# Modulation tiles stored transposed and summed on VectorE, the opening and the load order rearranged, narrow projections merged

## The chip, the cores and the metric

The kernel runs on one core of a Trainium2 chip, in one launch. The metric is the device time of a launch in microseconds (us). The core's engines run side by side and synchronise by semaphores: TensorE (PE, matmuls into PSUM), VectorE (DVE), ScalarE (ACT), GpSimd (POOL), and SyncE (SP), which here issues every DMA, in the order of the program.

## What is computed

Two small transformer blocks of float32, on 256 tokens of width 1024. The first has two layers whose norms are modulated by a condition vector `c`; the second adds 16 meta tokens, a differential attention and 16 experts.

```python
cond = jax.nn.silu(c)
for layer in range(2):
    mod = cond @ ada_w[layer] + ada_b[layer]                  # (1024) x (1024, 6144)
    sh1, sc1, g1, sh2, sc2, g2 = jnp.split(mod, 6, axis=-1)
    h = modulate(rms_norm(x, mix_norm[layer]), sh1, sc1)      # y * (1 + sc1) + sh1
    y = ab_mixer(h, ...) if layer == 0 else cd_mixer(h, ...)
    x = x + g1 * y
    h = modulate(rms_norm(x, ffn_norm[layer]), sh2, sc2)
    x = x + g2 * swiglu(h, ffn_w1[layer], ffn_w2[layer])
# then second_block(x, ...): attention and convolution, 16 experts of 34 tokens each
```

In `ab_mixer`, `h @ w_in` gives gated linear attention inputs (`gq, gk, gv`, a gate of rank 16, `gr`), attention inputs (`dq, dk, dv`), and an indexer (`iq` with 8 heads, one shared key `ik` of 64, and 8 weights `iw` per token). The indexer's scores pick 64 keys per token; q and k are normed and rotated; the outputs are projected back.

## The kernel before

Everything is kept transposed, features on partitions and tokens along the free dimension: `X` and `H` are 8 tiles of 128 x 272, of which 256 columns are the tokens. Weights come through a ring of five slots `RING_T` of 2 MB each (128 x 4096). The list `LOADS` fixes which weight goes into which slot: entry j takes slot j mod 5. `sp_weight` (L2314) issues a load on SP after it has waited until the slot's last user is done (`w.prev.left`); since SP is one queue, a load that waits also holds up all loads behind it.

The 6144 modulation values of a layer are made in 12 tiles of 512, `("ada", layer, i)`: tiles 0 and 1 are the shift of the first norm, 2 and 3 its scale, 4 and 5 the gate of the mixer, 6 and 7 the shift of the second norm, 8 and 9 its scale, 10 and 11 the gate of the FFN. A tile holds 8 groups of 128 inputs x 512 outputs. `dve_ada` multiplies each group by the silu of `c` (one value per partition, `CND`) and adds into `ACC` (L1610, then L1613). Then `pe_ada` sums over the partitions with four matmuls against a column of ones (L473, 16 instructions for two tiles), and `dve_mod` adds the bias from PSUM (L1623). For the first four tiles PE takes the last group itself (L506).

The order of the work is written out by hand for each engine, in `pe_ab`, `act_ab`, `dve_ab`, `pool_ab` and in `sync_program`. In the opening, VectorE first makes the angles of the rotation (L1675 to L1696), then the four first tiles with the statistic of the first norm between them, then scales x (L1640); ScalarE adds the shift (L1167); PE does the narrow projections: gate (L519, 16 columns), the indexer key twice into two halves of the partitions (L524), gate expansion (L530), and the token weights (L535, 32 matmuls of 8 columns). Then come the wide projections in chunks of 128 outputs (`pe_chunk`, L418, 16 instructions for 256 tokens): iq, gqk, gv (L427), and then dq, dk, dv and gr between the steps of the two attentions. On VectorE the long selection of the 64 keys is L1771 and L1773, eight rounds; the scores are L1756 to L1763; norms are L1561 to L1583. The out projection (`pe_out_proj`) has a `hook` by which PE and VectorE do tiles 6 to 9 between its chunks, and the residual is L1657. The FFNs (L741 to L743 and L760 to L762) sum more tiles in between (`EXTRA`), as does the second layer's mixer.

Of the kernel before, what the change touches and what calls it, by code (L numbers as in the profile page):

```python
# [6 lines left out]
F32 = mybir.dt.float32  # L7
# [29 lines left out]
    ("ident", 128), ("ones", 128), ("rot128", 128), ("rot64", 128), ("tri16", 128), ("tri", 128),  # L37
    ("after", 128), ("before", 128), ("tmask", 128), ("smask", 128), ("cmask", 256), ("inv", 2),
    ("eps", 1), ("one", 1), ("iota", CAP),
# [3 lines left out]
    ("c", 8), ("ada_b", 96), ("mix_norm", 16), ("ffn_norm", 16), ("gla_out", 1), ("dsa_q", 1), ("dsa_k", 1),  # L43
# [50 lines left out]
def ada_steps(n):
    return KC - 1 if n < 4 else KC


def ada_done(n):
    return sum(ada_steps(i) for i in range(n % 2, n + 1, 2))
# [8 lines left out]
HS = {"mix0": 0, "ffn0": 8, "mix1": 16, "ffn1": 24}  # L108
# [115 lines left out]
def bc(ap, *shape):  # L224
# [22 lines left out]
class Kit:  # L247


    def __init__(self, nc, A, out):  # L250
# [4 lines left out]
        self.HWC = sbt("HWC", [128, KC * L + KC * SMALL + LN], F32)  # L255
# [3 lines left out]
        self.CL = self.HWC[:, KC * (L + SMALL):]  # L259
# [53 lines left out]
class AbViews:  # L313
    def __init__(self, s):
# [19 lines left out]
        self.IW = s.take(2, 8)  # L334
# [3 lines left out]
        self.G1 = self.TR[:, 3, 0:T]  # L338
        self.PT = self.bufs[0].rearrange("p a (b c) -> p (a b) c", c=128)
# [125 lines left out]
def pe_ada(nc, k, n):  # L465

    key = ("ada", *ADAS[n])
    early = n < 4
    u = k.banks[key] if early else pe_bank(nc, k, key)
    acc = k.ACC[:, n % 2, :]  # L470
    nc.tensor.wait_ge(k.sem[f"ada{n % 2}"], ada_done(n))
# [3 lines left out]
    ins.then_inc(u.full, 1)  # L475
    if early:

        k.ring[key].left = (u.full, u.n)
        k.banks.drop(key)


def pe_out_proj(nc, k, name, keys, mix, n, stat, hook):
    for i in range(2):
        w = k.ring[keys[i]]
        nc.tensor.wait_ge(w.sem, w.n)
        for j in range(4):
            u = pe_chunk(nc, k, (name, "out", 4 * i + j), w.v(KC, 512), j, mix, n)
            stat.upto(min(max(4 * i + j - stat.lag, 0), KC) if 4 * i + j < 7 else 7)
            hook(4 * i + j)
        w.left = (u.full, u.n)  # L490
    stat.upto(KC)


def pe_ab(nc, k):
    pe, s, v, P, ring = nc.tensor, k.sem, k.ab, k.banks, k.ring
    ones = k.cc("ones")
    pe.wait_ge(s["vecs"], 16)
    pe.wait_ge(s["consts"], 16)
    pe.wait_ge(s["cond"], 1)

    for n in range(4):
        w = ring["ada", 0, n]
        u = pe_bank(nc, k, ("ada", 0, n), hold=True)
        pe.wait_ge(w.sem, w.n)
        for j in range(4):
            pe.matmul(u.t[:, j:j + 1], w.v(KC, 512)[:, 7, j * 128:(j + 1) * 128], k.CND[:, 7:8],  # L506
                      start=j == 0, stop=False, skip_group_check=True)
        if n == 0:
            stat = PeStat(nc, k, "mix0", M)
            stat.upto(KC)  # L510
        else:
            pe_ada(nc, k, n - 1)
    pe_ada(nc, k, 3)

    u = pe_bank(nc, k, "g1")
    pe.wait_ge(s["small"], 16)
# [10 lines left out]
    pe.wait_ge(P["g1"].taken, P["g1"].done)  # L527
# [74 lines left out]
    pe_ada(nc, k, ADA_AT[0, 4])  # L602
    pe_ada(nc, k, ADA_AT[0, 5])
# [102 lines left out]
    pe_out_proj(nc, k, "ab", [("abo", 0), ("abo", 1)], v.MIX, T, stat, hook)  # L706
# [6 lines left out]
def pe_ffn(nc, k, layer):  # L713
# [73 lines left out]
def pe_cd(nc, k):  # L787
# [17 lines left out]
    pe_ada(nc, k, ADA_AT[1, 4])  # L805
    pe_ada(nc, k, ADA_AT[1, 5])
# [11 lines left out]
    pe_ada(nc, k, ADA_AT[1, 6])  # L818
    pe_ada(nc, k, ADA_AT[1, 7])
# [37 lines left out]
    pe_out_proj(nc, k, "cd", [("cdo", 0), ("cdo", 1)], v.MIX, T, stat, hook)  # L857


def pe_diff(nc, k):  # L860
# [1659 lines left out]
```

## Time and profile before

| | us |
|---|---|
| median of three timed runs | 1958.38 (1957.93 to 1961.32) |
| the profiled execution | 1954.44 |
| its span, first to last instruction | 1953.0 |
| PE busy (share) | 1716.3 (88%) |
| VectorE busy (share) | 642.9 (33%) |
| ScalarE busy (share) | 370.8 (19%) |
| GpSimd busy (share) | 28.8 (1%) |
| DMA, mean over the span | 295 GB/s |
| first layer's mixer ends, first FFN starts | about 245 |

Shares are means over stages with different limits, so they don't say what a stage waits for. The timeline tells when an instruction ran and, in square brackets, how long its engine had been idle and what released it; the chain of waits is followed back from the last instruction of the kernel.

### The profile page before, as it was taken

To read this page: it belongs to the slowest core of one execution; us is meant where nothing else is said; L and a number is where in the kernel's file an instruction comes from. 1 tells how busy PE (TensorE), PEld (TensorE's weight loads), DVE (VectorE), ACT (ScalarE), POOL (GpSimd) and SP (SyncE) were. 2 spreads that over 40 slices of the span, in tenths; PEclk is the share of its full clock that TensorE was granted. 3 is DMA by queue.
4 is the path that set the end of the run, shared out by engine and by line. 5 is a ranking of instruction groups with operands and counts; after the bars stand their busy time and mean duration, and the time that the engine had idled before them with its cause. 6 is when DMAs were issued, how large, how long until landed. Compare 5 with 4: busy or idle time off the path is not lost.

```text
span 1953.0 us, 21048 instructions
## 1 busy us (share of the span) xinstructions
PE 1716.3 (88%) x8993; PEld 1034.4 (53%) x8993; DVE 642.9 (33%) x1230; ACT 370.8 (19%) x649; POOL 28.8 (1%) x35
## 2 busy tenths in 40 slices
PE   4999889999989999999798889878888887797787
PEld 3776789997679999757532323222222222232222
DVE  6156678755657554344300100101001010010102
ACT  2112243333324333132100000000000000000001
POOL 0101000000000000100001000000000000000000
PEclk7999989999899999999879999989998899999989
DMA  9342457744554656123539989999999999999995
GB/s 393 139 184 87 191 219 289 313 175 173 220 194 149 250 185 237 43 96 120 215 133 413 428 363 390 425 429 428 426 426 427 428 422 428 427 422 428 426 424 243
DMA packets 43309, 576.48 MB, mean 295 GB/s; under 512 B 4673, under 2 KB 6482, under 8 KB 6866
## 3 DMA queue, kind: packets, MB, share of 16 engines
q1 hardware_dynamic: 43218, 575.15, 71.5%
q8 instruction: 72, 1.18, 0.2%
q14 instruction: 19, 0.16, 0.0%
HBM read 574.08 MB, written 1.05 MB: 294 GB/s over the span
## 4 chain that ended last, share of the span: by engine, by line
PE 68%; DMA 23%; DVE 6%; ACT 2%; issue 1%; SPq 0%; DVEq 0%; ACTq 0%
DMA RING_T<-in_w_up 22%; PE P L1046 17%; PE P L418 12%; PE P L1067 5%; PE P L741 4%; PE P L742 4%; PE P L743 4%; PE P L427 3%; PE P L760 2%; PE P L762 2%; PE P L761 2%; PE P L1025 2%; DVE ACC L1613 2%; PE P L1083 2%; PE P L445 1%; PE P L473 1%
## 5 line engine op out<-in xcount | busy, mean ns | idle before, releaser
L1046 PE MATMUL P<-RING_T,SCR 128*34 128x512 f32 x1008 | 485.2, 638 | 128.4 <-DMA RING_T<-in_w_up 128.3
L1047 PE MATMUL P<-RING_T,SCR 128*34 128x512 f32 x992 | 479.1, 640 | 0.0
L1046 PEld LDWEIGHTS P<-RING_T,SCR 128*34 128x34 f32 x1008 | 114.8, 119 | 446.1 <-issue 445.6
L2170 DVE TENSOR_TENSOR SCR<-P,SCR 34x512 f32<-34x512 f32 x64 | 44.3, 693 | 785.5 <-ACT SCR L1515 785.5
L1067 PE MATMUL P<-RING_T,SCR 128*34 128x512 f32 x512 | 230.5, 598 | 18.3 <-DMA RING_T<-in_w_down 18.3
L1068 PE MATMUL P<-RING_T,SCR 128*34 128x512 f32 x512 | 230.4, 598 | 0.0
L741 PE MATMUL P<-SCF 128*128 128x256 f32 x704 | 204.9, 291 | 15.6 <-DVE SCF L1890 10.9
L418 PE MATMUL P<-HWC,RING_T 128*128 128x256 f32 (+1 forms) x832 | 197.5, 396 | 7.9 <-ACT HWC L1167 4.1
L742 PE MATMUL P<-SCF 128*128 128x256 f32 x704 | 202.5, 288 | 0.0
L743 PE MATMUL P<-SCF 128*128 128x256 f32 x704 | 202.4, 287 | 0.0
L418 PEld LDWEIGHTS P<-HWC,RING_T 128*128 128x128 f32 x832 | 162.0, 196 | 40.9 <-issue 14.3
L1515 ACT ACTIVATE SCR<-P 34x512 f32<-34x512 f32 x64 | 37.8, 591 | 611.6 <-PE P L1047 611.6
L741 PEld LDWEIGHTS P<-SCF 128*128 128x128 f32 x704 | 138.1, 196 | 17.6 <-issue 11.7
L1067 PEld LDWEIGHTS P<-RING_T,SCR 128*34 128x34 f32 x512 | 53.6, 112 | 164.8 <-issue 123.9
L742 PEld LDWEIGHTS P<-SCF 128*128 128x128 f32 x704 | 138.7, 197 | 0.0
L743 PEld LDWEIGHTS P<-SCF 128*128 128x128 f32 x704 | 138.5, 197 | 0.0
L1867 DVE TENSOR_TENSOR SCF<-RING_T,SCF 128x1024 fp32r<-128x1024 f32 x88 | 106.1, 1221 | 39.9 <-ACT SCF L1310 39.9
L1047 PEld LDWEIGHTS P<-RING_T,SCR 128*34 128x34 f32 x992 | 113.2, 119 | 0.0
L1613 DVE SCALAR_TENSOR_TENSOR ACC<-RING_T,CND,ACC 128x512 f32<-128x512 f32 x164 | 111.6, 746 | 0.9
L1310 ACT ACTIVATE SCF<-RING_T 128x1024 fp32r<-128x1024 f32 x88 | 91.9, 1053 | 66.0 <-PE P L762 35.0
L760 PE MATMUL P<-SCF 128*128 128x256 f32 x352 | 100.7, 286 | 0.0
L761 PE MATMUL P<-SCF 128*128 128x256 f32 x352 | 99.6, 283 | 0.0
(246 smaller groups left out, 1793.8 us busy)
## 6 DMA issues: line engine op xcount, KB each, us to landing
RING_T<-in_w_down SPq DMA_DIRECT2D x64, 2048.0 KB, 13.2
RING_T<-in_w_gate SPq DMA_DIRECT2D x63, 2048.0 KB, 17.2
RING_T<-in_w_up SPq DMA_DIRECT2D x62, 2048.0 KB, 12.4
RING_T<-in_ada_w SPq DMA_DIRECT2D x24, 2048.0 KB, 12.3
RING_T<-in_ffn_w SPq DMA_DIRECT2D x22, 2048.0 KB, 8.5
RING_T<-in_ffn_w SPq DMA_DIRECT2D x22, 1024.0 KB, 4.9
RING_T<-in_ab_w_in SPq DMA_DIRECT2D x7, 2048.0 KB, 12.7
RING_T<-in_w_in SPq DMA_DIRECT2D x6, 2048.0 KB, 7.4
```

Of the source, the lines that this page charges most:

```text
L418: ins = nc.tensor.matmul(u.t[:, 0:n], wap[:, c, j * 128:(j + 1) * 128], h[:, c, :], start=c == 0, stop=c == KC - 1)
L741: pe.matmul(o, wh, v.HH[:, 0, c, :], start=c == 0, stop=False)
L742: pe.matmul(o, wh, v.HH[:, 1, c, :], start=False, stop=False)
L743: ins = pe.matmul(o, wl, v.HH[:, 0, c, :], start=False, stop=c == KC - 1)
L760: pe.matmul(o, wh, v.HR[:, f % NHD, 0, :], start=f == 0 and m % 2 == 0, stop=False, skip_group_check=True)
L761: pe.matmul(o, wh, v.HR[:, f % NHD, 1, :], start=False, stop=False, skip_group_check=True)
L1046: pe.matmul(u.t[0:CAP, :], xs, wg.v(KC, 512)[:, c, :], start=c == 0, stop=c == KC - 1)
L1047: ins = pe.matmul(u.t[64:64 + CAP, :], xs, wu.v(KC, 512)[:, c, :], start=c == 0, stop=c == KC - 1)
L1067: pe.matmul(u.t[0:CAP, :], hs, w.v(4, 1024)[:, c, 0:512], start=first, stop=end)
L1068: ins = pe.matmul(u.t[64:64 + CAP, :], hs, w.v(4, 1024)[:, c, 512:1024], start=first, stop=end)
L1613: nc.vector.scalar_tensor_tensor(out=acc, in0=src, scalar=k.CND[:, c:c + 1], in1=acc, op0=ALU.mult, op1=ALU.add).then_inc(sem, 1)
L1867: nc.vector.tensor_tensor(lo, w.up()[:, :, z, j * 128:(j + 1) * 128], hi.bitcast(F32), ALU.subtract).then_inc(k.sem["lo"], 1)
```

## The change

1. Each modulation tile is stored transposed in HBM, outputs on partitions, as 4 groups of 128 outputs x 1024 inputs. The silu of `c` lies as a row of 1024 in every partition (`CB`). One VectorE instruction multiplies a group by `CB` and sums it along the free dimension (`accum_out`) into `MOD`. TensorE no longer takes part, `ACC` and the hooks are gone.
2. For the first four tiles, the fourth group is multiplied by GpSimd and summed by ScalarE. GpSimd also multiplies x by the norm's factor, and ScalarE applies scale and shift in one step, after the tiles.
3. The scale tiles (2 and 3) are loaded first. The angles and the sine tables come after the four tiles. `CB`, x and a piece of the constants are loaded ahead.
4. Gate and token weights are one projection with 40 columns; the token weights are then transposed. The indexer key is projected once with its columns doubled.
5. In the first mixer, tiles 4 to 9 are loaded earlier and summed at earlier places on VectorE. In the other stages the tiles keep their place, without the matmuls.

```diff
-LOADS = [("ada", 0, i) for i in range(4)]
-LOADS += ["iq", "gqk", ("ada", 0, 4), ("ada", 0, 5), "gv", "dq", "dk", "dv", "gr", ("ada", 0, 6), ("ada", 0, 7)]
-LOADS += [("abo", 0), ("abo", 1), ("ada", 0, 8), ("ada", 0, 9)]
+LOADS = [("ada", 0, i) for i in (2, 3, 0, 1)]
+LOADS += ["iq", "gqk", ("ada", 0, 4), "gv", ("ada", 0, 5), ("ada", 0, 6), "dq", ("ada", 0, 7), "dk", ("ada", 0, 8), "dv"]
+LOADS += [("ada", 0, 9), "gr", ("abo", 0), ("abo", 1)]
...
-def pe_ada(nc, k, n):
...
-    for j in range(4):
-        ins = nc.tensor.matmul(u.t[:, j:j + 1], acc[:, j * 128:(j + 1) * 128], k.cc("ones")[:, 0:1],
-                               start=not early, stop=True, skip_group_check=True)
...
     for c in range(KC):
         pe.wait_ge(s["hn"], HN["mix0"] + c + 1)
-        ins = pe.matmul(u.t[0:16, 0:T], k.WS[:, c, 0:16], k.HX[:, c, :], start=c == 0, stop=c == KC - 1)
+        ins = pe.matmul(u.t[0:40, 0:T], v.WN[:, c, 0:40], k.HX[:, c, :], start=c == 0, stop=c == KC - 1)
...
-    for half in range(2):
-        for c in range(KC):
-            ins = pe.matmul(u.t[64 * half:64 * half + 64, 0:T], k.WS[:, c, 16:80], k.HX[:, c, :], start=c == 0, stop=c == KC - 1)
+    for c in range(KC):
+        ins = pe.matmul(u.t[:, 0:T], v.WN[:, c, 40:168], k.HX[:, c, :], start=c == 0, stop=c == KC - 1)
...
-        for c in range(KC):
-            ins = pe.matmul(u.t[:, 8 * i:8 * i + 8], k.HX[:, c, i * 128:(i + 1) * 128], k.WS[:, c, 80:88], start=c == 0, stop=c == KC - 1)
+        ins = pe.transpose(u.v(2, 8)[:, i, :], v.IWR[0:8, i * 128:(i + 1) * 128], k.cc("ident")[0:8, 0:8])
...
-    act_shift(nc, k, "mix0", 0)
+    for n in range(ADA_SHARED):
+
+        layer, i = ADAS[n]
+        act.wait_ge(s["ada_p"], n + 1)
+        w = k.ring["ada", layer, i].v(4, D)[:, 3, :]
+        act.activation(w, w, ACT.Copy, accum_out=k.MOD[:, layer, 4 * i + 3:4 * i + 4]).then_inc(s["ada_a"], 1)
...
+        act.activation(h, h, ACT.Identity, bias=k.shift(0, 0)[:, c:c + 1], scale=k.SA[:, 0, c:c + 1]).then_inc(s["hn"], 1)
...
+def dve_ada_sums(nc, k, n, groups):
+
+
+    layer, i = ADAS[n]
+    w = k.ring["ada", layer, i]
+    if groups[0] == 0:
+        nc.vector.wait_ge(w.sem, w.n)
...
+    for g in groups:
+        src = w.v(4, D)[:, g, :]
+        nc.vector.scalar_tensor_tensor(out=src, in0=src, scalar=1.0, in1=k.CB[:, :], op0=ALU.mult, op1=ALU.mult,
+                                       accum_out=k.MOD[:, layer, 4 * i + g:4 * i + g + 1]).then_inc(k.sem["ada"], 1)
...
     score(1, 1)
+    dve_ada(nc, k, 0, 9)
     dve.wait_ge(s["score"], at[0])
     select(1, 0)
...
+    for n in range(ADA_SHARED):
+        layer, i = ADAS[n]
+        w = k.ring["ada", layer, i]
+        pool.wait_ge(w.sem, w.n)
+        if n == 0:
+            pool.wait_ge(s["cond"], 1)
+        pool.tensor_tensor(w.v(4, D)[:, 3, :], w.v(4, D)[:, 3, :], k.CB[:, :], ALU.mult).then_inc(s["ada_p"], 1)
+        if n == 1:
+
+            pool.wait_ge(s["rs"], rms_done("mix0"))
+            pool.wait_ge(P["rms", "mix0"].full, P["rms", "mix0"].n)
+            for c in range(KC):
+                pool.tensor_tensor(k.H[:, c, M:L], k.X[:, c, M:L], k.RS[:, 0, 0:T], ALU.mult).then_inc(s["xr"], 1)
```

On VectorE in the opening, before (a row is an instruction with its output, its inputs and its shape; `RS` is the norm's factor, `SA` the scale, `HWC` the tensor that holds `H`):

```order
L1696 TENSOR_SCALAR SCR<-SCR 128x512 [waits angle]
L1610 TENSOR_SCALAR ACC<-RING_T,CND 128x512 [waits weights0,cond]
L1613 SCALAR_TENSOR_TENSOR ACC<-RING_T,CND,ACC 128x512 [waits ada0] x6
L1561 TENSOR_SCALAR RS<-P 128x256 [waits full1]
...
L1613 SCALAR_TENSOR_TENSOR ACC<-RING_T,CND,ACC 128x512 [waits ada1] x6
L1623 TENSOR_TENSOR MOD<-P,VC 128x4 [waits full3]
L1623 TENSOR_TENSOR MOD<-P,VC 128x4 [waits full4]
L1632 SCALAR_TENSOR_TENSOR SA<-MOD,VC 128x8 [waits taken4,taken3]
L1640 SCALAR_TENSOR_TENSOR HWC<-X,SA,RS 128x256 [waits rs,sa]
```

and of the changed kernel, the same place:

```order
L1565 SCALAR_TENSOR_TENSOR RING_T,MOD<-RING_T,CB 128x1024 [waits barrier_Pool_Activation_PE_DVE_SP_release,cond,weights0]
L1565 SCALAR_TENSOR_TENSOR RING_T,MOD<-RING_T,CB 128x1024 x2
L1519 TENSOR_SCALAR RS<-P 128x256 [waits full0]
...
L1576 TENSOR_TENSOR MOD<-MOD,VC 128x4 [waits ada_a,ada,vecs]
L1565 SCALAR_TENSOR_TENSOR RING_T,MOD<-RING_T,CB 128x1024 [waits weights1]
L1565 SCALAR_TENSOR_TENSOR RING_T,MOD<-RING_T,CB 128x1024 x2
L1576 TENSOR_TENSOR MOD<-MOD,VC 128x4 [waits ada_a,ada]
L1592 SCALAR_TENSOR_TENSOR SA<-MOD,VC 128x8 [waits mod]
L1565 SCALAR_TENSOR_TENSOR RING_T,MOD<-RING_T,CB 128x1024 [waits weights2,sa]
...
L1643 CAST SCR<-SCR 128x256 [waits consts,pos]
```

Three sums per tile stand on VectorE, each bias addition waits for ScalarE (`ada_a`), the scaling of x has left the engine, and the angles begin after the fourth tile. On GpSimd in the changed kernel:

```order
L2174 TENSOR_TENSOR RING_T<-RING_T,CB 128x1024 [waits cond,weights0]
L2174 TENSOR_TENSOR RING_T<-RING_T,CB 128x1024 [waits weights1]
L2180 TENSOR_TENSOR HWC<-X,RS 128x256 [waits full0,rs]
L2180 TENSOR_TENSOR HWC<-X,RS 128x256 x7
L2174 TENSOR_TENSOR RING_T<-RING_T,CB 128x1024 [waits weights2]
```

Before, GpSimd had no product until the indexer queries. On VectorE at the selection, the changed kernel (L1730 and L1732 are the selection, L1771 and L1773 before) has

```order
L1722 SCALAR_TENSOR_TENSOR SCR<-SCR 128x256 [waits score] x3
L1565 SCALAR_TENSOR_TENSOR RING_T,MOD<-RING_T,CB 128x1024 [waits weights0]
L1565 SCALAR_TENSOR_TENSOR RING_T,MOD<-RING_T,CB 128x1024 x3
L1576 TENSOR_TENSOR MOD<-MOD,VC 128x4 [waits ada]
L1730 MAX SCR<-SCR 128x8 [waits score]
```

where the selection followed the scores at once before. The load of that tile stands on SP behind dv's, and takes slot 0 from dq:

```order
L2261 DMA RING_T<-in_ada_w 128x4096 [waits mod]
L2261 DMA RING_T<-in_ab_w_in 128x4096 [waits mod]
L2261 DMA RING_T<-in_ada_w 128x4096 [waits full2]
L2261 DMA RING_T<-in_ab_w_in 128x4096 [waits mod]
L2261 DMA RING_T<-in_ab_w_out 128x4096 [waits full6]
```

These are tile 8, dv, tile 9, gr and the first half of the out projection; before, tiles 6 to 9 stood behind gr and behind the out projection's weights.

## Rows read from the trace of the kernel before

**Rows 1.** The page: span, and shares of the chain that ended last.
```profile
span 1953.0 us, 21048 instructions
...
PE 68%; DMA 23%; DVE 6%; ACT 2%; issue 1%; SPq 0%; DVEq 0%; ACTq 0%
```

**Rows 2.** Timeline of the opening: start us, us, engine, line, operation.
```profile
15.21 1.84 PE L506 MATMUL P<-CND,RING_T 128*128 128x1 f32 x8 [15.21 <-DMA RING_T<-in_ada_w]
...
44.98 5.25 PE L519 MATMUL P<-HWC 128*16 128x256 f32 x16 [1.75 <-ACT HWC L1167]
50.16 6.31 PE L524 MATMUL P<-HWC 128*64 128x256 f32 x32
...
61.05 15.75 PE L418 MATMUL P<-HWC,RING_T 128*128 128x256 f32 x64
```

**Rows 3.** Timeline from 76 to 82, GpSimd and VectorE.
```profile
77.39 4.09 POOL L2223 TENSOR_TENSOR SCR<-SCR 128x512 f32<-128x512 f32 x3 [59.63 <-ACT SCR L1134]
...
78.36 0.85 DVE L1717 TENSOR_TENSOR SCR<-SCR 128x512 f32<-128x512 f32 x1 [17.98 <-ACT SCR L1134]
79.13 1.76 DVE L1718 TENSOR_TENSOR SCR<-SCR 128x512 f32<-128x512 f32 x1
```

**Rows 4.** Groups by line and shape: busy, mean ns; last, one accumulator read.
```profile
L1613 DVE SCALAR_TENSOR_TENSOR ACC<-RING_T,CND,ACC 128x512 f32<-128x512 f32 x164 | 111.6, 746 | 0.9
L1867 DVE TENSOR_TENSOR SCF<-RING_T,SCF 128x1024 fp32r<-128x1024 f32 x88 | 106.1, 1221 | 39.9 <-ACT SCF L1310 39.9
L1563 DVE TENSOR_TENSOR SCR<-SCR 128x512 f32<-128x512 f32 x10 | 6.9, 693 | 13.6 <-ACT SCR L1143 13.6
L2223 POOL TENSOR_TENSOR SCR<-SCR 128x512 f32<-128x512 f32 x6 | 8.0, 1346 | 145.3 <-DVE SCR L1583 85.7 <-ACT SCR L1134 59.6
L2223 POOL TENSOR_TENSOR SCR<-SCR,HWC 128x272 f32<-128x272 f32 x8 | 6.1, 764 | 366.0 <-ACT SCR L1134 366.0
196.09 0.19 ACT L1276 ACTIVATION_READ_ACCUMULATOR SCR<-SCR 128x1 f32 x1
```

**Rows 5.** Windows: length, busy by engine, PE's granted clock, DMA, GB/s.
```profile
46.00:48.00 2.00, 2.00 (x6) 0.67 (x5) 0.99 (x3) 1.62 (x5) 0.00 (x0) 0.50 1.01 422
...
62.00:64.00 2.00, 2.00 (x6) 1.63 (x5) 0.00 (x0) 0.00 (x0) 0.00 (x0) 0.50 0.00 0
```

**Rows 6.** Chain of waits, 108 to 143: start, us, what.
```profile
110.13 1.88 PE P L473 x16
...
121.11 7.10 PE P L418 x32
```

**Rows 7.** Timeline of VectorE, 120 to 157.
```profile
124.45 0.43 DVE L1771 MAX8 SCR<-SCR 128x8 f32<-128x256 f32 x1
...
132.65 0.29 DVE L1777 TENSOR_TENSOR SCR<-SCR,C 128x128 f32<-128x128 f32 x1
...
143.93 1.52 DVE L1763 SCALAR_TENSOR_TENSOR SCR<-SCR 128x128 f32<-128x128 f32 x4 [3.95 <-ACT SCR L1134]
145.36 0.69 DVE L1561 TENSOR_SCALAR SCR<-P 128x512 f32<-128x512 f32 x1
...
156.26 0.69 DVE L1561 TENSOR_SCALAR SCR<-P 128x512 f32<-128x512 f32 x1 [1.04 <-PE P L457]
```

**Rows 8.** Out projection: PE's start in the timeline, then the chain of waits.
```profile
207.70 10.60 PE L418 MATMUL P<-SCR,RING_T 128*128 128x256 f32 x48 [0.73 <-issue]
...
214.03 7.52 DMA RING_T<-in_ada_w
...
243.45 0.40 DVE X L1657
...
245.15 0.43 DVE RS L1561
```

**Rows 9.** Chain of waits in the first FFN, then PE's timeline in the second mixer.
```profile
298.13 1.68 PE P L473 x16
...
518.44 2.71 PE L473 MATMUL P<-C,ACC 128*128 128x1 f32 x16 [1.49 <-DVE ACC L1613]
```

More of the change, by code:

```diff
@@ L36 @@
 CONSTS = [
-    ("ident", 128), ("ones", 128), ("rot128", 128), ("rot64", 128), ("tri16", 128), ("tri", 128),
-    ("after", 128), ("before", 128), ("tmask", 128), ("smask", 128), ("cmask", 256), ("inv", 2),
-    ("eps", 1), ("one", 1), ("iota", CAP),
+    ("ones", 128), ("eps", 1), ("one", 1), ("inv", 2), ("ident", 128), ("rot128", 128), ("rot64", 128), ("tri16", 128), ("tri", 128),
+    ("after", 128), ("before", 128), ("tmask", 128), ("smask", 128), ("cmask", 256),
+    ("iota", CAP),
 ]
@@ L91, with ada_own @@
 ADA_AT = {x: n for n, x in enumerate(ADAS)}
[L94 to L99, printed above, removed]
+ADA_SHARED = 4
+def ada_own(n):
+    return 4 * (n + 1) - min(n + 1, ADA_SHARED)
 RMS = ["mix0", "dq0", "dq1", "go0", "go1", "dk0", "dk1", "ffn0", "mix1", "sq0", "sq1", "sk0", "sk1", "ffn1", "mix2"]
@@ L333, in __init__ @@
         self.OT = s.take(4, T)
[L334 removed]
+        self.IW, self.IWR = s.take(2, 8), self.OT[:, 0, :]
         self.m8 = [s.take(8), s.take(8)]
@@ L496, in pe_ab @@
     ones = k.cc("ones")
[L497 to L516, printed above, removed]
+    pe.wait_ge(s["ones_in"], 16)
+    PeStat(nc, k, "mix0", M).upto(KC)
+    u = pe_bank(nc, k, "narrow", takers=2)
+    pe.wait_ge(s["narrow"], 16)
     for c in range(KC):
         pe.wait_ge(s["hn"], HN["mix0"] + c + 1)
-        ins = pe.matmul(u.t[0:16, 0:T], k.WS[:, c, 0:16], k.HX[:, c, :], start=c == 0, stop=c == KC - 1)
+        ins = pe.matmul(u.t[0:40, 0:T], v.WN[:, c, 0:40], k.HX[:, c, :], start=c == 0, stop=c == KC - 1)
     ins.then_inc(u.full, 1)
     u = pe_bank(nc, k, "ik")
-    for half in range(2):
-        for c in range(KC):
-            ins = pe.matmul(u.t[64 * half:64 * half + 64, 0:T], k.WS[:, c, 16:80], k.HX[:, c, :], start=c == 0, stop=c == KC - 1)
+    for c in range(KC):
+        ins = pe.matmul(u.t[:, 0:T], v.WN[:, c, 40:168], k.HX[:, c, :], start=c == 0, stop=c == KC - 1)
     ins.then_inc(u.full, 1)
     u = pe_bank(nc, k, "gate", takers=2)
-    pe.wait_ge(P["g1"].taken, P["g1"].done)
+    pe.wait_ge(P["narrow"].taken, P["narrow"].done - 1)
     pe.wait_ge(s["gup"], 16)
@@ L972, in pe_experts @@
     u = pe_bank(nc, k, "router")
+    pe.wait_ge(s["small"], 16)
     for c in range(KC):
         pe.wait_ge(s["hn"], HN["ffn2"] + c + 1)
-        ins = pe.matmul(u.t[0:16, 0:L], k.WS[:, c, 88:104], k.H[:, c, :], start=c == 0, stop=c == KC - 1)
+        ins = pe.matmul(u.t[0:16, 0:L], k.WS[:, c, :], k.H[:, c, :], start=c == 0, stop=c == KC - 1)
     ins.then_inc(u.full, 1)
@@ L1626, in dve_adjusted, with dve_ada @@
+    k.ring["ada", layer, i].left = (k.sem["mod"], n + 1)
+def dve_ada(nc, k, layer, *tiles):
+    for i in tiles:
+        n = ADA_AT[layer, i]
+        dve_ada_sums(nc, k, n, range(4))
+        dve_mod(nc, k, n)
 def dve_adjusted(nc, k, layer, part):
-    for i in (6 * part + 2, 6 * part + 3):
-        u = k.banks["ada", layer, i]
-        nc.vector.wait_ge(u.taken, u.done)
+    nc.vector.wait_ge(k.sem["mod"], max(ADA_AT[layer, 6 * part + 2], ADA_AT[layer, 6 * part + 3]) + 1)
     w = k.vv("ffn_norm" if part else "mix_norm", layer * 8, layer * 8 + 8)
@@ L1893, in dve_ffn @@
     used = 0
-    extra, due = list(EXTRA[layer]), []
+    extra = list(EXTRA[layer])
     for i in range(12):
@@ L1922, in dve_ffn @@
         if i < 11 and extra and i % 2:
-            due = [extra.pop(0), extra.pop(0)]
-            dve_ada(nc, k, [ADA_AT[a] for a in due])
+            dve_ada(nc, k, *extra.pop(0))
+            dve_ada(nc, k, *extra.pop(0))
     gate = k.gate(layer, 1)
-    for a in (10, 11):
-        dve.wait_ge(P["ada", layer, a].taken, P["ada", layer, a].done)
+    dve.wait_ge(s["mod"], ADA_AT[layer, 11] + 1)
     for c in range(KC):
@@ L2492 @@
     w = g["ab_w_in"][0]
-    small = np.concatenate([w[:, 1024:1040], w[:, 3600:3664], w[:, 3664:3672], g["w_router_2"][0]], 1)
+    keys = w[:, 3600:3664]
+    narrow = np.concatenate([w[:, 1024:1040], np.zeros((D, 16), np.float32), w[:, 3664:3672], keys, keys], 1)
     arrays = {
```

246 lines of the change are left out of this document (98 added, 148 removed).

## The prediction

> **What bounds the kernel now.** I read the page first. In the chain that ended last, PE holds 68% and the DMA 23% [rows 1]; the DMA share is the expert stage, where loads of w_up end the waits. That stage takes weights at a fixed rate and starts when PE frees the ring slots of the block before it, so a microsecond saved on PE's path ahead of it moves the whole stage forward. The change touches only what lies before it: the first layer's mixer (to about 245 us), the two FFNs and the second mixer.
>
> Then the timeline of the opening [rows 2]. PE waits until 15.21 for the first modulation tile and starts the first projection at 44.98; VectorE's tile sums stand between. The narrow projections then fill PE until the wide ones start at 61.05. Third, the chain of waits from 108 to 157: PE alone sets the pace up to the end of the fourth dq chunk at 128.21 (the row at 121.11 and its 7.10) [rows 6], and VectorE takes over with the norm of dq at 145.36 [rows 7]. Fourth, the out projection: it starts at 207.70, but its residuals wait behind tile sums (one of them 7.52 for its load), and the statistic is ready only at 245.15 [rows 8]. Last, the ones-matmuls of the tiles (L473): 1.68 us per pair on PE's path [rows 9].
>
> **The new tile sum.** Before, a tile is eight VectorE instructions of 128x512 (0.746 us each, [rows 4]) and four matmuls. After, it is four of 128x1024 with two SBUF inputs and an accumulated output. No row shows that form. The nearest is L1867, 128x1024 with two SBUF inputs: 1.221. An accumulator read on ScalarE is 0.19 and overlaps partly [rows 4]; from below it costs nothing, from above 0.19. I take 1.34 for one and 4 x 1.34 + 0.16 = 5.5 for a tile with its bias addition. Eight steps of 0.746 with some overlap cost 5 to 6 before: on VectorE alone the change is about even.
>
> **Opening.** The first tile has 3.8 MB up to its end ahead in the queue, where it had 4.2; at 422 GB/s [rows 5] that is 1.0 us, so it lands near 14.2 and the others 4.9 apart. The angles leave the front, but GpSimd enters: four products of 128x1024 and eight x·rs products of 128x256. From L2223 (1.346 for 512 elements, 0.764 for 272 [rows 4]) I estimate 2.4 to 2.6 and 0.73. Can they run beside VectorE? No [rows 3]: while GpSimd does three products from 77.39 on, VectorE's L1718 takes 1.76 where that shape takes 0.693 in L1563 [rows 4]. The two take turns, whole instructions at a time: GpSimd's second product fills the gap, VectorE's comes behind it, and GpSimd's third (a 128x256) behind that, to the end at 81.48. So I add both engines' work: 14.2 + VectorE 12 x 1.34 = 16.1, statistic and small additions 2.5, GpSimd 4 x 2.45 + 8 x 0.73 = 15.6. That makes 48.4, about 48 with what overlaps PSUM reads and the ScalarE steps. Then ScalarE writes the last four h tiles in under 2 us (estimate), and PE finishes the merged gate and token-weight projection near 50.3, where L519 ended at 50.2: no gain from the tiles. What follows is shorter. L524 was 6.31 for 32 instructions [rows 2]; the key columns doubled in one 128-wide pass take one chunk's time, 3.45 (three chunks in 10.60 with 0.2 of the pipe's end, [rows 8]). Gate 1.1 as before. The 32 small token-weight matmuls between 57.5 and 61.05 become two transposes, 0.3. The wide projections start near 55.2: **5.8 earlier**. With the two engines not blocking each other it would be about 13.5.
>
> The Trainium skill, page "SBUF — State Buffer", section "Who interferes with whom", says just this: a VectorE instruction with two SBUF inputs and a GpSimd instruction that reads SBUF exclude each other for a whole instruction. By that rule, the trace agrees in the 1.76 of L1718. This rule speaks against the change, which puts both kinds side by side.
>
> PE's granted clock was half (0.50) at 46 to 48 and again at 62 to 64 in the middle of steady work [rows 5]; such a dip of 3 us costs 1.5. I leave it as before.
>
> **From 55 us to the dq norm.** PE's order is the same except for 1.88 us of L473 at 110.13 [rows 6], so dq's fourth chunk ends at 128.21 - 5.8 - 1.9 = 120.5. Tiles 4 to 8 of the first layer sit in VectorE's gaps; tile 8 delays the state updates by a few us, which PE meets only at about 121. But tile 9 is loaded into dq's own ring slot, and SP can issue it only when the fourth chunk is done. On VectorE it stands **ahead of the long top-k selection**. Behind it queue the selection, the scores of the first block, the ReLU that waits for their buffer, and the dq norm. From the chunk's end: load 7.5 (as 214.03, [rows 8]), tile 5.5, selection 8.5 (124.45 to 132.94), scores 1.5, ReLU 0.9 (estimate: two 128x256 activations), scores 1.4 [rows 7] = 25.3. Before it was 145.36 - 128.21 = 17.2. This gives back 8.1 of the 7.7: the norm starts at 145.8, **+0.4**. What covered the early gain is gone here. PE is far ahead by now, so the 1.04 that VectorE waited for PE at 156.26 goes: **-1.0**.
>
> **Out projection.** Sums, load wait, and four bias additions leave it. From 207.70 on (all times still those of before): eight chunks of 3.45, and between them four statistic matmul pairs of 0.43 (an eighth of a chunk): 237.0; then the tail from last residual to the statistic, 245.15 - 243.45 = 1.7 [rows 8]: 238.8. **-6.3**.
>
> **Later stages.** The first FFN has three L473 groups of 1.68 on the chain (one shown, the others at 334.47 and 370.81): -5.0. The second mixer: one at 492.89 (1.68), then 1.49 of waiting and 2.71 at 518.44 [rows 9], one at 573.57 (1.68): -7.6. VectorE's tile pair there runs from 507 to 518 and the masks behind it end before the value projection on PE does, so it stays covered; an extra 1 us would still be hidden. Second FFN, 633.63: -1.7. VectorE has room in both FFNs.
>
> **Sum:** +0.4 - 1.0 - 6.3 - 5.0 - 7.6 - 1.7 = -21.2. The profiled execution took 1954.44 for a span of 1953.0; it becomes 1933.2. The three timed runs have a median of 1958.38, 3.9 above it, so I forecast 1958.4 - 21.2 = **1937 us**. A measurement of this kernel can tell about 0.2% (3.9 us) from no change.
>
> **Rivals.**
> - **The engines do not block each other in the opening.** For it: the blocked instruction of [rows 3] is a single case. Against: its length fits taking turns to 0.1 us. Wide projections start 13.5 earlier instead of 5.8; all the rest stays, since the 25.3 hangs on the dq chunk: -29, 1929 us. Chance 0.2.
> - **PE's clock takes the gain.** PE idles from about 13 to 44 us where it had small matmuls, and after an idle stretch it ran at half clock [rows 5]. If the merged projections and the first wide chunk stay at 1.2 GHz for 8 to 14 us more: +4 to 7, so about 1943. Chance 0.15.
> - **Slower: the accumulating form runs at half rate.** No row has it. Then 2.4 instead of 1.34. The opening gets 12 x 1.1 longer, tile 9 4.4, the second mixer's pair 8.8 less 1 hidden: +25, 1962 us. It decides from about 0.9 us extra per instruction. Against it: a ScalarE accumulation costs only 0.1 to 0.2. Chance 0.08.
> - **Hidden anyway.** If the expert stage's DMA bound did not move with PE, nothing would be seen: 1958. Against: the loads are released by PE's instructions. Chance 0.05.
>
> **Numbers.** The forecast has 0.52. Faster by over 0.2%: 0.52 + 0.2 + 0.15 = 0.87; same 0.05; slower 0.08. The range must leave out at most 2 in 10: it holds the forecast with ±7 for load times and clock dips, the first rival and the second: 1924 to 1950.
>
> **What would show it.** In the profile after: GpSimd products and VectorE's 128x1024 sums alternate up to about 48 us, with VectorE's taking up to 1.3 plus 2.4; the wide projections start near 55; VectorE idles about 5 us for a load of in_ada_w near 121 to 128, then tile 9, then the selection up to about 142; dq's norm near 146; the FFN's first statistic near 238; no L473 group anywhere, and the later stages shorter by 5.0, 7.6 and 1.7. I am wrong if the sum instruction is not 1.2 to 1.4, if GpSimd's products overlap with it, or if the wait for tile 9 is absent.

## The result and the profile after

| | before | after |
|---|---|---|
| median of the timed runs | 1959.28 (1957.93 to 1961.32, 4 runs) | 1916.09 (1914.45 to 1916.94, 4 runs) |
| profiled execution, its span | 1954.44, 1953.0 | 1914.45, 1912.8 |

The ratio is 0.9778 (95%: 0.9761 to 0.9795): the kernel is 43 us faster, twice the 21 that I forecast, and outside my range. Ratios and medians here leave out one execution of the run g2 below: it took 3348.61 us, against 1905.73 to 1913.88 of the other four, and no trace shows why.

The page of after, against [rows 1]: the chain has the same owners, in nearly the same shares.

```profile
span 1912.8 us, 20481 instructions
...
PE 67%; DMA 24%; DVE 6%; ACT 2%; issue 1%; POOL 1%; SPq 0%; DVEq 0%; ACTq 0%
```

So the page alone says nothing of where 40 us went. What does is a line that both kernels have in every stage: VectorE's first instruction of a norm (L1561 before, L1519 after). Its start, read from both timelines, cuts the span into stages; the first two rows are read from PE, and as before's 61.05 is the timeline's figure where its chain of waits has 61.20, they carry an error of some 0.15:

| up to | before | after | stage shorter by | my forecast |
|---|---|---|---|---|
| wide projections start | 61.05 | 50.33 | 10.7 | 5.8 |
| end of the fourth dq chunk | 128.21 | 113.98 | 3.5 | 1.9 |
| norm of dq | 145.36 | 138.96 | -7.8 | -8.1 |
| statistic of the first FFN | 245.15 | 231.41 | 7.3 | 7.3 |
| statistic of the second mixer (first FFN) | 457.86 | 438.56 | 5.6 | 5.0 |
| statistic of the second FFN (second mixer) | 580.65 | 551.18 | 10.2 | 7.6 |
| statistic of the attention block (second FFN) | 791.04 | 759.75 | 1.8 | 1.7 |
| statistic of the experts (attention block) | 951.87 | 919.92 | 0.7 | 0 |
| last statistic (experts) | 1943.98 | 1903.78 | 8.3 | 0 |
| sum | | | 40.2 | 21.2 |

Four stages are off: the opening (4.9), the way to dq (1.6), the second mixer (2.6) and the experts (8.3), where I had put nothing.

The opening in the timeline of after, VectorE, GpSimd, ScalarE and PE (columns as in [rows 2]); the last row is from the chain of waits:

```profile
13.61 1.23 DVE L1565 SCALAR_TENSOR_TENSOR RING_T<-RING_T,CB 128x1024 f32<-128x1024 f32 x1 [13.61 <-DMA RING_T<-in_ada_w]
14.76 0.08 DVE L1565 DVE_READ_ACCUMULATOR RING_T<-RING_T,CB 128x1 f32 x1
14.76 3.35 DVE L1565 SCALAR_TENSOR_TENSOR RING_T<-RING_T,CB 128x1024 f32<-128x1024 f32 x1
...
13.65 3.38 POOL L2174 TENSOR_TENSOR RING_T<-RING_T,CB 128x1024 f32<-128x1024 f32 x1 [12.61 <-DMA RING_T<-in_ada_w]
18.73 2.75 POOL L2174 TENSOR_TENSOR RING_T<-RING_T,CB 128x1024 f32<-128x1024 f32 x1 [1.69 <-DMA RING_T<-in_ada_w]
...
22.66 1.22 DVE L1565 SCALAR_TENSOR_TENSOR RING_T<-RING_T,CB 128x1024 f32<-128x1024 f32 x1
...
23.81 1.73 DVE L1565 SCALAR_TENSOR_TENSOR RING_T<-RING_T,CB 128x1024 f32<-128x1024 f32 x1
...
22.75 11.38 POOL L2180 TENSOR_TENSOR HWC<-X,RS 128x256 f32<-128x256 f32 x8 [1.28 <-DVE RS L1525]
34.09 4.64 POOL L2174 TENSOR_TENSOR RING_T<-RING_T,CB 128x1024 f32<-128x1024 f32 x2
...
42.22 0.16 DVE L1576 TENSOR_TENSOR MOD<-MOD,VC 128x4 f32<-128x4 f32 x1
...
40.55 5.00 PE L488 MATMUL P<-HWC,SCR 128*40 128x256 f32 x16 [26.23 <-ACT HWC L1136]
45.48 3.72 PE L492 MATMUL P<-HWC,SCR 128*128 128x256 f32 x16
...
50.33 14.01 PE P L419 x64
```

A sum alone takes 1.23 (its accumulator read 0.08 beside the next one; from start to start 1.15). With a GpSimd product in the way the same instruction takes 3.35, that is 1.2 and 2.15; with the small products 1.73. The engines do take turns. The last bias addition is at 42.2 where I had 48.4. Of these 6.2 us, 1.4 are lost again before the first projection ends, at 45.55: I had 1.9 between the two, and it took 3.3.

The chain of waits around tile 9:

```profile
106.86 7.12 PE P L419 x32
114.00 8.04 DMA RING_T<-in_ada_w
122.03 0.02 issue
122.06 4.68 DVE RING_T L1565 x8
...
126.93 0.35 DVE SCR L1730
...
136.78 0.67 ACT SCR L1078 x2
```

This is the wait that I had put there, row for row: dq's chunk ends, then the load, the tile, the selection, the scores and the ReLU. The norm follows at 138.96, 25.0 after the chunk.

### The profile page after: what moved, and what is told of

The parts are those of the page before. It is cut to its first block, busy times and chain, and to the rows that moved or that the text cites. A ratio compares the mean times of both kernels' runs of the same rounds, so it can differ in the third digit from the quotient of the medians.

```text
span 1912.8 us, 20481 instructions
## 1 busy us (share of the span) xinstructions
PE 1672.8 (87%) x8723; PEld 998.9 (52%) x8723; DVE 634.1 (33%) x1218; ACT 378.8 (20%) x659; POOL 51.0 (3%) x47
## 4 chain that ended last, share of the span: by engine, by line
PE 67%; DMA 24%; DVE 6%; ACT 2%; issue 1%; POOL 1%; SPq 0%; DVEq 0%; ACTq 0%
DMA RING_T<-in_w_up 22%; PE P L990 16%; PE P L419 13%; PE P L1011 6%; PE P L700 4%; PE P L701 4%; PE P L702 4%; PE P L428 3%; PE P L721 2%; PE P L720 2%; PE P L719 2%; PE P L969 2%; PE P L1027 2%; DVE RING_T L1565 1%; DMA RING_T<-in_ada_w 1%; PE P L446 1%
## 5 line engine op out<-in xcount | busy, mean ns | idle before, releaser
L1565 DVE SCALAR_TENSOR_TENSOR RING_T<-RING_T,CB 128x1024 f32<-128x1024 f32 x92 | 112.4, 1277 | 28.8 <-DMA RING_T<-in_ada_w 28.7
```

Source lines behind the costliest of these rows:

```text
L1565: nc.vector.scalar_tensor_tensor(out=src, in0=src, scalar=1.0, in1=k.CB[:, :], op0=ALU.mult, op1=ALU.mult, accum_out=k.MOD[:, layer, 4 * i ...
```

## The experiments

Ratios are to the kernel before on the same chip.

### Is the gain in the experts the kernel's, or the execution's?

**e1**: the kernel before again, no edit.

> The kernel before, unchanged, profiled again. It tests the part of the gain that no edit explains: from the last statistic of the attention block to the end of the kernel, the expert stage took 992.1 us in the trace of before (951.87 to 1943.98) and 983.9 us in that of after (919.92 to 1903.78), 8.2 us less, and a 16 KB DMA packet took 618 ns there against 614 ns. Theory A (where the tensors lie decides): this run shows 618 ns and about 992 us again, while the variants of after in the same job show 614 ns and 984 us. Theory B (the execution or the chip decides, not the kernel): this run and the variants of after agree within 0.2% of the packet time and within 2 us in the expert stage.

Ratio 0.9989 (0.9969 to 1.0008), and the expert stage took 992.2 us (960.23 to 1952.43), beside 992.1 the first time. The three variants of after in the same job took 985.3, 986.8 and 985.8. A 16 KB packet in the DMA records took 613 ns in the median and 620 at the 90th percentile here, 611 and 611 in each variant. Theory B is out: the kernel decides. (The means that the expectations compare, 618 against 614 ns, hold a few much longer packets; median and 90th percentile do not.) What differs for the experts is where things lie. The small tensors ahead of the ring changed in size, so the ring starts at byte 57536 of a partition before (224 x 256 + 192) and at 58624 after (229 x 256).

**f1**: before, two tensors moved behind the ring, which then starts at 51200 = 200 x 256.

```diff
-        self.C = sbt("C", [128, CN], F32)
...
-        self.CND = sbt("CND", [128, 8], F32)
...
         self.ring = Ring(nc)
+        self.C = sbt("C", [128, CN], F32)
+        self.CND = sbt("CND", [128, 8], F32)
```

> The kernel before with one thing changed: two small tensors (C and CND) are allocated behind the ring of weights instead of ahead of it, so that the ring starts at byte 51200 of each partition, a multiple of 256, where it started at 57536 (192 beyond one); in after it starts at 58624, again a multiple of 256, by the accident of which small tensors the change removed. No instruction changes. Theory A (the ring's start decides the DMA rate of the expert stage): packets of 16 KB take 614 to 616 ns instead of 618, the expert stage 984 to 987 us instead of 992.1, the time falls by 5 to 8 us (ratio 0.996 to 0.9975). Theory B (the place of the inputs in HBM, or which small loads there are, decides): nothing changes, 992 us and ratio 1.000. The Trainium skill, page DMA: Bandwidth & Descriptors, section How a descriptor splits into AXI transactions, says that a descriptor that does not start at a multiple of 256 bytes costs additional beats; that would be theory A.

**f2**: after, the ring moved off the multiple (g3 and g4 the same with 16 and 32 in place of 48).

```diff
+        self.PAD = sbt("PAD", [128, 48], F32)
         self.ring = Ring(nc)
```

> After with 192 unused bytes per partition allocated ahead of the ring, so that it starts 192 beyond a multiple of 256 as it did before. No instruction changes. Theory A: packets of 618 ns and an expert stage of 991 to 993 us instead of 983.9 to 986.8; the time rises by 5 to 8 us against after (ratio to before 0.981 to 0.982 instead of 0.978). Theory B: 984 to 987 us and ratio 0.978.

> After with 64 unused bytes per partition ahead of the ring: it starts 64 beyond a multiple of 256. If only a multiple of 256 gives the faster transfers (as the 192 beyond in f2 had 618 ns and 990.4 us in the expert stage), this run has 618 ns and 990 to 992 us, and 6 us more than g1. If a multiple of 64 were enough, f2's 192 would have been fast too; so 64 should be slow.

> The same with 128 bytes: the ring starts 128 beyond a multiple of 256. Slow as f2 (618 ns, 990 to 992 us) if 256 is needed; fast as after (611 to 615 ns, 984 to 987 us) if a multiple of 128 is enough.

| kernel | ring starts beyond a multiple of 256 by | packet, median and 90th percentile, ns | expert stage, us | ratio |
|---|---|---|---|---|
| before, e1 | 192 | 613, 620 (both) | 992.1, 992.2 | 1, 0.9989 |
| f1 | 0 | 611, 611 | 987.3 | 0.9958 (0.9941 to 0.9974) |
| after, g1 | 0 | 611, 611 (both) | 983.9, 987.6 | 0.9778, 0.9775 |
| f2 | 192 | 613, 620 | 990.4 | 0.9814 (0.9797 to 0.9831) |
| g3 | 64 | 613, 620 | 991.8 | 0.9809 (0.9776 to 0.9842) |
| g4 | 128 | 612, 619 | 992.2 | 0.9803 (0.9770 to 0.9835) |

The stage's ends are the starts of two VectorE rows. In f1:

```profile
952.89 0.44 DVE L1561 TENSOR_SCALAR RS<-P 128x272 f32<-128x272 f32 x1 [1.28 <-PE P L445]
1940.21 0.42 DVE L1561 TENSOR_SCALAR RS<-P 128x256 f32<-128x256 f32 x1 [1.29 <-PE P L445]
```

in f2:

```profile
926.12 0.44 DVE L1520 TENSOR_SCALAR RS<-P 128x272 f32<-128x272 f32 x1 [1.28 <-PE P L447]
1916.55 0.42 DVE L1520 TENSOR_SCALAR RS<-P 128x256 f32<-128x256 f32 x1 [1.29 <-PE P L447]
```

And the rate in the 40 slices of the page, first before, then f1, then after:

```profile
GB/s 393 139 184 87 191 219 289 313 175 173 220 194 149 250 185 237 43 96 120 215 133 413 428 363 390 425 429 428 426 426 427 428 422 428 427 422 428 426 424 243
```

```profile
GB/s 392 131 194 87 179 232 277 315 186 158 236 182 147 254 184 241 51 87 130 216 106 417 431 365 402 429 426 430 424 430 429 431 428 430 430 426 423 424 431 240
```

```profile
GB/s 398 217 220 179 107 199 331 240 155 246 223 173 265 166 168 197 88 88 131 177 224 424 367 428 404 429 430 427 430 431 430 431 430 431 430 424 429 428 430 242
```

The best slices of before stand at 427 to 429, those of f1 and after at 430 to 431: 0.6% on a stage that waits only for DMA. Moving nothing but the ring gives before 0.4% and takes 0.3 to 0.4% from after (g3 and g4 are two timed runs each, and their intervals touch that of g1; their expert stages don't). Theory A holds; of the four starts tried only the multiple of 256 was fast. Over nine executions with it the stage took 986.2 on average (983.9 to 990.0), over five without 991.7 (990.4 to 992.2). So 5.6 of the 8.3 is the ring; the other 2.7 is no more than the spread among executions. The Trainium skill, page "DMA: Bandwidth & Descriptors", section "How a descriptor splits into AXI transactions", says that a descriptor which doesn't start at a multiple of 256 bytes fetches from the multiple below it, and that the unused bytes cost beats. Its words and examples are of reads. The runs agree in the direction for rows of 16 KB written to SBUF, with up to 9 ns on 611 for a packet; no run here shows beats, so that this is the mechanism isn't shown.

### Do GpSimd and VectorE take turns in the opening?

**e3**: one wait added, so that GpSimd's eight products of x run without VectorE's sums beside them.

```diff
     dve_mod(nc, k, 0)
+    dve.wait_ge(s["xr"], KC)
     dve_ada_sums(nc, k, 1, range(3))
```

> After, but VectorE waits before the second tile's sums until GpSimd has finished its eight products of x. If the engines take turns, the products took 1.42 each only since VectorE's sums stood between them; alone they need about 0.5, are done near 27 instead of 34.1, the sums then run unblocked, and the wide projections start within 1.5 us of 50.3 (time 1915 to 1918). If the 1.42 is GpSimd's own pace, VectorE stands still for 11.4 us and everything comes 7 to 11 us later, 1923 to 1927.

The timeline of e3 (the last row is from the chain of waits):

```profile
22.52 5.50 POOL L2181 TENSOR_TENSOR HWC<-X,RS 128x256 f32<-128x256 f32 x8 [1.28 <-DVE RS L1525]
27.97 5.62 POOL L2175 TENSOR_TENSOR RING_T<-RING_T,CB 128x1024 f32<-128x1024 f32 x2
...
28.05 3.34 DVE L1565 SCALAR_TENSOR_TENSOR RING_T<-RING_T,CB 128x1024 f32<-128x1024 f32 x1 [5.53 <-POOL HWC L2181]
31.32 3.35 DVE L1565 SCALAR_TENSOR_TENSOR RING_T<-RING_T,CB 128x1024 f32<-128x1024 f32 x1
...
51.18 8.83 PE P L419 x40
```

The products took 5.50 instead of 11.38. VectorE stood still for 5.53 and the wide projections start 0.85 later. The blocked sums now stand behind the two long products instead, 3.35 each. The rival had 7 to 11. The ratio is 0.9790 (0.9775 to 0.9805), whose interval overlaps after's; the median of 1919.76 is a little above the 1915 to 1918 expected.

**e2**: GpSimd and ScalarE out of the tiles; VectorE also multiplies x.

```diff
-ADA_SHARED = 4
+ADA_SHARED = 0
...
-    dve_ada_sums(nc, k, 0, range(3))
+    dve_ada_sums(nc, k, 0, range(4))
...
+    for c in range(KC):
+        dve.tensor_tensor(k.H[:, c, M:L], k.X[:, c, M:L], k.RS[:, 0, 0:T], ALU.mult).then_inc(s["xr"], 1)
```

> After, with the opening's GpSimd products and ScalarE sums given to VectorE: four sums per tile there, and x times the norm's factor as eight 128x256 products on VectorE. If the engines take turns (my theory), GpSimd's share costs VectorE as much as it saves: last bias addition near 40.0 (22.3 for the statistic less 0.9, eight products 3.4, twelve sums of 1.15, and 1.0 of small steps) against 42.2, wide projections start about 2.3 us earlier than 50.3, time 1912 to 1915 on a chip where after gives 1916. If GpSimd really did its work beside VectorE, taking it away costs VectorE 4 x 1.15 + 3.4 = 8 us, and the wide projections start 5 to 8 us later, 1921 to 1924. Every sum should now take 1.22, none 1.73.

The timeline of e2:

```profile
20.89 2.77 DVE L1633 TENSOR_TENSOR HWC<-X,RS 128x256 f32<-128x256 f32 x8
...
35.82 1.22 DVE L1565 SCALAR_TENSOR_TENSOR RING_T<-RING_T,CB 128x1024 f32<-128x1024 f32 x1
...
38.23 0.16 DVE L1576 TENSOR_TENSOR MOD<-MOD,VC 128x4 f32<-128x4 f32 x1
...
47.63 14.08 PE L419 MATMUL P<-HWC,RING_T 128*128 128x256 f32 x64
```

With 4 tiles of 4 sums on one engine the last bias addition is at 38.2 instead of 42.2, and the wide projections start 2.6 earlier: without the help the engine is faster. (I had expected 40.0 and 2.3; the products of x took 2.8 and not 3.4.) The ratio is 0.9786 (0.9771 to 0.9800), though, the same as after's: the forecast gain in time didn't come. By the start of the out projection, 199.11 against 199.98, only 0.9 of the 2.6 is left; 1.2 went between the fourth norm (151.49 against 154.10) and the fifth (167.10 against 168.54), the rest behind the norms. What happens in the projection is the question of g1 below.

### What does tile 9's place cost?

**e4**: its sums moved from ahead of the selection to the end of the mixer.

```diff
     score(1, 1)
-    dve_ada(nc, k, 0, 9)
     dve.wait_ge(s["score"], at[0])
...
+    dve_ada(nc, k, 0, 9)
     dve.wait_ge(s["mod"], ADA_AT[0, 5] + 1)
```

> After, with tile 9's sums moved from ahead of the long selection to behind the product that ends the mixer, where VectorE idles for the first output chunk (199 to 204). My prediction put 13 us of load and sums between the fourth dq chunk and the dq norm. If that holds, the norm comes at about 134 instead of 138.96 (PE's statistic at 131.6 to 133.3 is then the limit), PE's waits of 2.87 and 1.74 before the next norms shrink, and the first FFN starts 4 to 5 us earlier: 1911 to 1912. Rival: the norms behind it wait for PE anyway and the gain is under 1 us; or the residuals behind the moved sums come late and take the gain back: 1915 to 1917.

The norm of dq came at 133.90, 5.1 earlier, and the out projection started at 196.28 instead of 199.98. Its first four chunks then took 16.11 where after's took 14.05, and the FFN's statistic came at 229.76, 1.65 earlier. Ratio 0.9777 (0.9754 to 0.9799): no gain that can be measured, as the second rival had it.

**g1**: after again, in one job with **g2**, which has both e2's and e4's edits (as **f4** had).

> After with both edits of the earlier job: the opening's sums all on VectorE, and tile 9 behind the mixer. Each alone brought its gain up to the output projection (wide projections 2.7 earlier; projection started 3.7 earlier) and then lost 2 us there, where its first four chunks took 16.1 to 16.2 us instead of 14.05 with TensorE's clock at half. If the gains add up to the start of the projection it starts 5 to 6 earlier than 199.98, and with the half clock in it the first FFN's statistic comes at 227 to 228 instead of 231.41: 1912 to 1914, ratio 0.976. If TensorE's clock takes all of it, 1916 and 0.978.

> After, unchanged, as the reference of this job: 1914 to 1919, ratio 0.978, expert stage 984 to 987 us, packets 611 ns (median).

> The kernel of f4 again (the opening's sums on VectorE alone, tile 9 behind the mixer), now beside after on the same chip. f4 gave 0.9754 (0.9736 to 0.9771) where after had given 0.9778 on another chip. If the gain is real the ratio to before is again 0.975 to 0.976, and 4 to 6 us lie between this run and g1; if it was the chip, under 2 us.

The out projection in the timeline of g1, two of its windows (columns as in [rows 5]), and a window of the first profile of after:

```profile
201.30 16.55 PE L419 MATMUL P<-SCR,RING_T 128*128 128x256 f32 x64 [0.73 <-issue]
```

```profile
204.00:206.00 2.00, 2.00 (x6) 1.64 (x5) 0.00 (x0) 0.00 (x0) 0.00 (x0) 0.50 0.00 0
...
208.00:210.00 2.00, 2.00 (x11) 1.77 (x10) 0.09 (x1) 0.42 (x1) 0.00 (x0) 1.00 0.00 0
```

```profile
194.00:196.00 2.00, 2.00 (x12) 2.00 (x11) 0.52 (x1) 1.97 (x3) 0.00 (x0) 0.50 0.09 37
```

This is after itself, unchanged, with the half clock (0.50, which is 1.2 GHz) in the same four chunks. In the first profile of after they ran at full clock in 14.05. The dip was there too, but earlier, at 194 to 196, in the small matmuls of the softmax part; so it isn't that the clock fell in one execution and not in the other. What differs is where the stretch at half clock falls, and inside the projection it is worth 2.5 us. Without e2's and e4's edits it fell there in two of seven profiles (g1 and f2, 16.55 and 16.63; after, e3, f3, g3 and g4 have 14.05), with one or both of them in four of four (16.10 to 16.73). So the edits aren't needed for it, but it isn't excluded that they move it there.

Set beside g1, which has the dip in the same place and its FFN statistic at 235.22, e2 is 2.5 earlier (232.72), e4 5.5 (229.76), g2 7.1 (228.16). But 1.2 of each is g1's opening, where the clock rose later: its first projection (L488) took 6.32 from 40.46 on, and 5.00 in the first profile of after. Beside that profile (231.41) e2 is 1.3 later and e4 1.65 earlier. For e2 and e4 alone a gain isn't shown; both together do give one in the timed runs. f4 measured 0.9754 (0.9736 to 0.9771) and g2 0.9745 (0.9718 to 0.9771), beside 0.9775 (0.9752 to 0.9797) of g1. On one chip the medians are 1913.2 (four runs) and 1918.26: 5.1 us, as expected. The intervals of the ratios just overlap, but each of g2's four is below each of g1's five, and f4 gave the same on another chip; this is the fastest version of the study.

### What did the column matmuls cost in the later stages?

**f3**: they are back at their seven places behind the first mixer, reading `CB`, their results unused.

```diff
+def pe_dummy(nc, k, layer, *tiles):
+    for i in tiles:
+        u = pe_bank(nc, k, ("ada", layer, i), takers=0)
+        nc.tensor.wait_ge(k.sem["mod"], ADA_AT[layer, i] + 1)
+        for j in range(4):
+            ins = nc.tensor.matmul(u.t[:, j:j + 1], k.CB[:, j * 128:(j + 1) * 128], k.cc("ones")[:, 0:1],
+                                   start=True, stop=True, skip_group_check=True)
+        ins.then_inc(u.full, 1)
```

> After with the matmuls against a column of ones put back on TensorE at their seven old places in the first FFN (three), the second mixer (three) and the second FFN (one), each place 8 matmuls of one column in two banks that wait until the tiles are summed; their results are not used. My forecast's price was 1.68 us a place, 1.49 of waiting and 1.0 more at one of them: +5.0 in the first FFN, +7.6 in the second mixer, +1.7 in the second FFN. The trace showed that after was shorter by 5.6, 10.2 and 1.8. Theory A: the mixer's 2.6 beyond my sum is TensorE's clock, which was at half for 10 us right behind the column matmuls at 518 in before and was not in after; then the half clock comes back here and the mixer is longer by 9 to 10. Theory B: the half clock there comes from something else, and the mixer is longer by 5 to 8. Total 1929 to 1934 on a chip where after gives 1916 (ratio 0.985 to 0.987).

The three stages got longer by 5.4, 8.9 and 1.8 against after; ratio 0.9865 (0.9849 to 0.9882). In the second mixer, the timeline of f3:

```profile
498.93 1.06 PE L784 MATMUL P<-SCR 128*128 128x256 f32 x2
...
505.80 1.02 PE L471 MATMUL P<-C,CB 128*128 128x1 f32 x8 [0.86 <-DVE MOD L1596]
506.69 8.81 PE L428 MATMUL P<-RING_T,HWC 128*128 128x512 f32 x16
```

and the same matmuls in after:

```profile
490.21 0.60 PE L765 MATMUL P<-SCR 128*128 128x256 f32 x2
...
494.32 7.03 PE L428 MATMUL P<-RING_T,HWC 128*128 128x512 f32 x16
```

Before, the first 16 matmuls of the value projection behind [rows 9]'s 518.44 took 9.68. A window of before inside them, and one of after:

```profile
524.00:526.00 2.00, 2.00 (x3) 0.73 (x3) 1.38 (x6) 0.00 (x0) 0.00 (x0) 0.50 0.99 426
```

```profile
498.00:500.00 2.00, 2.00 (x6) 0.85 (x5) 1.90 (x6) 0.00 (x0) 0.00 (x0) 1.00 1.04 410
```

So 2.65 of the 10.2 is the half clock in those 16 matmuls. They took 9.68, 9.95 and 9.77 in the three profiles of before's kernel (before, e1, f1), 8.81 in f3 and 7.03 in all ten others. The small matmuls ahead of them (L815 and L816 before) ran at half clock too, 4.4 instead of 2.7, but that cost nothing there: the column matmuls had to wait for VectorE's pair of tiles anyway. e1 shows it, where the small ones ran at full clock:

```profile
525.57 3.54 PE L473 MATMUL P<-C,ACC 128*128 128x1 f32 x16 [3.15 <-DVE ACC L1613]
```

So the wait that fell away was worth about 3.15; the profile of before showed 1.49 of it, since PE came late by the other 1.7. In after, 1.7 is lost again to waits of the pooling matmuls for VectorE. In f3 the path runs through VectorE's tiles and the column matmuls again, and the half clock is back in the 16 matmuls. That points to theory A, but the 8.9 lies just under its 9 to 10; it shows that the half clock comes back with the columns and their wait, not that they alone cause it. f3's expert stage took 990.0 with the ring on a multiple of 256 and a median packet of 611 ns; single longer packets raised the mean to 617. Why is open.

## Why the prediction was wrong

**Right.** The path through the stages that I costed. The tile form is about even on VectorE (4.7 a tile, before 10.07 for two, 508.81 to 518.88). The narrow projections went from 45.55 to 50.33 in 4.8, I had 4.9. Tile 9's wait took 25.0, I had 25.3. It gave back 7.8 as forecast (8.1); only, PE had won 14.2 by then and not 7.7, so the norm came 6.4 earlier and not 0.4 later. The out projection with the norms ahead of it gave 7.3, as forecast. Two FFNs: 5.6 and 1.8 for 5.0 and 1.7. The rival without blocking is refuted by e3, the half-rate sum by its 1.23; the clock was at half at 40 to 42 but did not stay low for 8 to 14 us (granted 1.00 at 50 to 52), and the experts moved with PE, so nothing was hidden.

**The sum "14.2 + 16.1 + 2.5 + 15.6" of the opening was mis-sized, by 4.9 in the end.** Adding both engines' work was right; the terms were too large. The tile landed at 13.6. A sum costs 1.15 from start to start and not 1.34, since the next starts under its tail: 13.8. GpSimd's share is four products at 2.32, as the last two show, and eight small ones in 5.50, as e3 shows: 14.8. That leaves nothing for the statistic and small additions (2.5): 13.6 + 13.8 + 14.8 = 42.2, which is the measured time. But that it agrees to 0.1 is in part luck. Half of the 2.5 does cost: from the end of GpSimd's second product at 21.5 to VectorE's next sum at 22.66 no product and no sum runs, 1.2 us. In exchange the eight small products took less than 5.50: from 22.66 to 34.1 they and six sums took 11.4, which leaves them 4.6.

Behind it, the h tiles and the end of the first projection took 3.3 where I had 1.9, with PE's granted clock at 0.50 at 40 to 42 and 0.66 at 42 to 44. That is why 6.2 in the sum are 4.9 at the wide projections.

**"I leave it as before", of the clock dip at 62 to 64, was a choice without ground.** It was gone (14.01 for the 64 matmuls in the chain of waits, 15.60 before), 1.6 us.

```profile
62.00:64.00 2.00, 2.00 (x11) 1.75 (x10) 0.00 (x0) 0.00 (x0) 0.00 (x0) 1.00 0.00 0
```

The execution doesn't decide this one. In the timelines the 64 matmuls took 15.75, 17.06 and 15.75 in the three profiles of before's kernel, and 14.08 in all eleven that have the merged projections. Which of the removed narrow matmuls did it, no run shows.

**The second mixer's -7.6 was mis-sized by 2.6.** I priced the wait at the 1.49 of its row; it was worth 3.15 (1.7 more). And I left the clock out, at half in the 16 matmuls behind the columns (2.65). Later waits for VectorE took back 1.7.

**"A stage that takes weights at a fixed rate" failed.** Its rate was not fixed: the change moved the ring by 1088 bytes, onto a multiple of 256, and the stage became 0.6% faster. That is 5.6 of the 19.0 that the sum was off, and 0.4% of the time by f1 and f2. It is the largest single miss. No view of the profile of before shows it; the sizes of the tensors do, and I had not followed what their removal moves.

**The base.** The two timed medians differ by 43.2, the spans by 40.2. Executions of before ranged from 1952 to 1966 in these jobs, so a sum made against one profile carries such an error too. The range of 1924 to 1950 allowed only for the opening and for dips; it should have held a term for the DMA-bound half of the span.

## What to carry to other kernels

Look where a ring of weights starts: in a stage bound by DMA, a multiple of 256 bytes was worth 0.4% here, free, and any change of a small tensor ahead of it can win or lose it unseen. GpSimd beside VectorE instructions with two SBUF inputs saves nothing: add both engines' times, and give the work to VectorE if it is the faster one for it (e2: the wide projections start 2.6 earlier, though a gain in time was measured only together with e4's edit). A tile loaded into the slot of the block just used, and summed ahead of a long VectorE piece, puts a whole load on the path; behind the mixer (e4) it let dq's norm start 5.1 earlier.

## What the hardware showed that I had not expected

- A VectorE instruction with accumulated output, 128x1024 with two SBUF inputs, takes 1.23 with 0.08 for the accumulator read, and 1.15 from start to start.
- A DMA packet of 16 KB takes 611 ns into a ring on a multiple of 256 bytes, and 611 to 620 into one 64, 128 or 192 bytes beyond.
- The stretch at half clock behind the softmax falls in different places in different executions of one kernel: four chunks took 14.05 in one profile of after and 16.55 in another. The FFN's statistic differed by 3.8 between the two, 2.5 of it from this and 1.2 from the first projection of the opening, behind a long idle stretch, where the clock rose later (6.32 for 5.00). That is more than many an edit is worth.
